# Cached keys turned by VectorE in 32x32 blocks instead of by TensorE, and fetched by one indirect transfer per slot from GpSimd's queue

## The reference

```python
D_MODEL, SEQ, DEC_BATCH, DEC_SEQ = 1024, 1024, 8, 4
PAST_LEN, PAGE_SIZE, N_HEADS, HEAD_DIM = 4096, 128, 8, 64      # 32 pages for each sample

def fox_sample(q, k, v, logf, k_past, v_past, logf_past):
    scale = HEAD_DIM ** -0.5
    d_new = lax.cumsum(logf, axis=1).transpose(0, 2, 1)
    rev = (lax.cumsum(logf_past, axis=1, reverse=True) - logf_past).transpose(0, 2, 1)
    sp = jnp.einsum('bqhd,bkhd->bhqk', q, k_past, preferred_element_type=jnp.float32) * scale
    sp = sp + d_new[:, :, :, None] + rev[:, :, None, :]
    ...  # sn: the same over the four new keys, causal
    p = jax.nn.softmax(jnp.concatenate([sp, sn], axis=-1), axis=-1)
    out = (jnp.einsum('bhqk,bkhd->bqhd', p[..., :n_past].astype(v_past.dtype), v_past)
           + jnp.einsum('bhqk,bkhd->bqhd', p[..., n_past:].astype(v.dtype), v))
```

## Time and profile before

| | |
|---|---|
| runs before | 2182.11, 2178.58, 2172.83 us, median 2178.58 us |
| profiled execution, span from first to last instruction | 2187.8 us |
| PE busy | 2010.4 us (92%) |
| DVE, ACT, POOL busy | 766.2 us (35%), 491.5 us (22%), 260.7 us (12%) |
| data moved | 458.72 MB, 210 GB/s over the span |
| from the scores of unit 0 to the end of slot 73 | 82.16 to 691.67 us |

### The profile page before, as it was taken

One profiled execution on the slowest core, in us unless ns is written; L12 is line 12 of the kernel. 1 busy time (PEld: TensorE's weight loads), 2 busy tenths in 40 slices (PEclk: granted clock), 3 DMA queues, 4 the chain that ended last, 5 costly groups with the idle time before them and its releaser, 6 DMA issues.

```text
span 2187.8 us, 34891 instructions
## 1 busy us (share of the span) xinstructions
PE 2010.4 (92%) x12990; PEld 1228.5 (56%) x12990; DVE 766.2 (35%) x1789; ACT 491.5 (22%) x1062; POOL 260.7 (12%) x402
## 2 busy tenths in 40 slices
PE   6999998989887999999999989998599999999994
PEld 4677765666654887788887446744333333333331
DVE  5221213555555572333333550623411111111115
ACT  3222222444331010111111021523122222221223
POOL 1101222322231000000000000000011111111110
PEclk9999999999998999999999999999799999999997
DMA  7546777987777022210111120304799999999976
GB/s 273 184 152 224 249 281 244 311 305 266 267 257 246 1 97 79 77 48 10 58 49 70 58 80 1 145 20 173 281 377 383 377 374 371 376 374 374 367 265 243
DMA packets 207153, 458.72 MB, mean 210 GB/s; under 512 B 18753, under 2 KB 48466, under 8 KB 206858
## 3 DMA queue, kind: packets, MB, share of 16 engines
q1 hardware_dynamic: 174410, 357.96, 46.4%
q0 software_dynamic: 32576, 98.53, 13.0%
HBM read 432.51 MB, written 32.17 MB: 212 GB/s over the span
## 4 chain that ended last, share of the span: by engine, by line
PE 82%; DMA 6%; DVE 4%; issue 3%; ACT 2%; SPq 2%; DVEq 1%; ACTq 0%; POOLq 0%
PE ps L1320 16%; PE ps L1625 10%; PE ps L1656 5%; PE ps L1380 5%; PE ps L1636 5%; PE ps L1121 5%; PE ps L1223 5%; PE ps L1409 4%; DMA kraw<-in_cache_k 3%; PE ps L1665 3%; PE ps L1093 3%; PE ps L1136 2%; PE ps L1498 2%; PE ps L1259 2%; PE ps L1234 2%
## 5 line engine op out<-in xcount | busy, mean ns | idle before, releaser
L1625 PE MATMUL ps<-gu,xgT 128*64 128x512 f32 x1024 | 228.5, 599 | 0.9 <-ACT xgT L1989 0.9
L1223 PE MATMUL ps<-consts,kraw 128*128 128x128 f32 x1024 | 141.6, 284 | 32.9 <-DMA kraw<-in_cache_k 27.7
L2985 POOL DMA_DIRECT2D vpage<-in_cache_v x232 | 125.0, 539 | 393.1 <-issue 385.2
L1320 PE MATMUL ps<-xnT,ring 128*128 128x264 f32 x672 | 162.1, 392 | 0.6 <-issue 0.6
L2264 DVE COPY kt<-ps 128x512 f32<-128x512 f32 x128 | 88.4, 691 | 202.6 <-PE ps L1223 201.9
L1223 PEld LDWEIGHTS ps<-consts,kraw 128*128 128x128 f32 x1024 | 116.3, 145 | 61.0 <-DMA kraw<-in_cache_k 30.7
L1625 PEld LDWEIGHTS ps<-gu,xgT 128*64 128x64 f32 x1024 | 71.1, 137 | 133.1 <-issue 130.0
L1320 PEld LDWEIGHTS ps<-xnT,ring 128*128 128x128 f32 x672 | 129.4, 193 | 23.8 <-issue 1.4
L1656 PE MATMUL ps<-wd,hidT_a 128*64 128x512 f32 x512 | 116.9, 598 | 19.6 <-ACT hidT_a L1999 12.7
L2874 DVE TENSOR_TENSOR sig_a<-ps,sig_a 128x256 f32<-128x256 f32 x32 | 13.6, 425 | 325.1 <-ACT sig_a L1993 325.1
L1762 ACT ACTIVATE kt<-ps 128x512 f32<-128x512 f32 x128 | 76.3, 596 | 191.9 <-PE ps L1223 190.0
(11 more groups left out here) (451 smaller groups left out, 3066.1 us busy)
## 6 DMA issues: line engine op xcount, KB each, us to landing
kraw<-in_cache_k SPq DMA_DIRECT2D x256, 256.0 KB, 4.1
gu<-in_w_expert_gate SPq DMA_DIRECT2D x32, 2048.0 KB, 23.4
gu<-in_w_expert_up SPq DMA_DIRECT2D x32, 2048.0 KB, 30.0
wd<-in_w_expert_down SPq DMA_DIRECT2D x31, 2048.0 KB, 8.3
vpage<-in_cache_v POOLq DMA_DIRECT2D x232, 256.0 KB, 4.9
ring<-in_w_in SPq DMA_DIRECT2D x12, 1024.0 KB, 9.1
yy<-y_d SPq DMA_DIRECT2D x16, 512.0 KB, 10.5
early<-in_w_in SPq DMA_DIRECT2D x6, 1024.0 KB, 10.1
```

Of the source, the lines that this page charges most:

```text
L1223: last = nc.tensor.transpose(bank(R.bank("kt", n, c))[:, j * PAGE:(j + 1) * PAGE], kraw[n % 2][:, j, c * P:(c + 1) * P], ident)
L1320: last = nc.tensor.matmul(bank(R.bank(name, f, q))[:, 0:QT], weight[:, k], src[:, k, cols], start=k == 0, stop=k == HK - 1)
L1625: last = nc.tensor.matmul(bank(0)[h * BA:(h + 1) * BA, :].rearrange("p (x n) -> p x n", x=2), src[:, k, 0:BA], weight[:, k, :, h * DE // 2 ...
L2985: pool.dma_start(vpage[value_place(n)][:, p, :], t["cache_v"][ds(page, 1)].rearrange("a s d -> (a s) d")).then_inc(v_in[value_place(n)], 16)
```

## The change

**Fetch.** `kraw[n % 2]` is filled by one indirect transfer on POOL's queue instead of four plain ones on SP's. A partition takes 8 KB in one piece: four consecutive tokens (c = 0..3) of all heads. Partition 32 j + s holds tokens 4 s to 4 s + 3 of page j. The row numbers `kidx` are loaded at the start by four small broadcasts and made by one DVE instruction.

**Turning.** `turn_keys` moves from PE to DVE: two instructions a unit, each turning 32x32 blocks of 128x1024 numbers from `kraw` into `kt`. The four tokens of a partition are interleaved again by the destination, so consecutive results lie 16 bytes apart. ACT and DVE no longer copy keys out of PSUM.

**Scores.** In `kt` the partitions 32 j to 32 j + 31 now hold 32 of a head's dimensions for page j's tokens, so the query operand is block-diagonal over the four pages (`qblk`, 32 columns, half of them zero), made for each sample by `spread_queries` (four small DVE copies). There are again 16 matmuls of 128x128 against 32 columns. A row of scores is now 4 x (head, query) + page instead of 32 x page + (head, query); `rev`, `sprob` and `snew` follow, and the sums over pages at the end are made on 8 partitions. The turned prompt probabilities are now all copied by ACT.

**Order.** POOL's list is now: keys of units 0 and 1, values of 0 and 1, keys 2 to 5, two small transfers for the new keys' terms, keys 6 to 13, and from then on values of n, keys of n+12. SP keeps the weights, `rev` and `negk`.

```diff
-        kt = [at(f"kt{s}", [P, KC, 4 * PAGE], a_ring + 16384 + s * 8192) for s in range(2)]
+        kt = [at(f"kt{s}", [P, NBLK, PAGE], a_ring + 16384 + s * 8192) for s in range(2)]
...
-        def load_keys(eng, n, p, page):
-
-            eng.dma_start(kraw[n % 2][:, p, :], t["cache_k"][ds(page, 1)].rearrange("a s d -> (a s) d")
-                          ).then_inc(k_in[n % 2], 16)
+        def load_keys(pool, n):
+
+            pool.indirect_dma_start(kraw[n % 2].rearrange("p c d -> p (c d)"), None,
+                                    t["cache_k"].rearrange("a (s c) d -> (a s) (c d)", c=4),
+                                    bass.IndirectOffsetOnAxis(ap=kidx[:, n:n + 1].bitcast(U32), axis=0)).then_inc(k_in[n % 2], 16)
...
             def sample_scores(n):
 
-                pe.wait_ge(side_ready, Q_READY)
-                R.read(pe, "kt", n, KC - 2), R.read(pe, "kt", n, KC - 1)
+                b = n // SU
+                pe.wait_ge(kt_ready, n + 1)
                 R.pe_free(pe, "sq", n)
-                for c in range(KC):
-                    for j in range(4):
-                        last = nc.tensor.matmul(bank(5)[j * QH:(j + 1) * QH, 0:PAGE], qnew[:, c, n // SU, :],
-                                                kt[n % 2][:, c, j * PAGE:(j + 1) * PAGE], start=c == 0, stop=c == KC - 1)
+                for x in range(4):
+                    first = x // 2 * 16
+                    for j in range(KC):
+                        last = nc.tensor.matmul(bank(5)[j * 32:(j + 1) * 32, 0:PAGE], qblk[b % 2][:, 2 * j + x % 2, first:first + 32],
+                                                kt[n % 2][:, 4 * j + x, :], start=x == 0, stop=x == 3)
                 last.then_inc(R.full, 1)
...
-            def copy_keys(n, c):
+            def turn_keys(n, half):
+
                 if n >= NSU:
                     return
-                if n >= 2:
-                    R.made(dve, "sq", n - 2)
-                R.made(dve, "kt", n, c)
-                nc.vector.tensor_copy(kt[n % 2][:, c, :], bank(R.bank("kt", n, c))).then_inc(R.by["dve"], 1)
+                if half == 0:
+                    dve.wait_ge(k_in[n % 2], 16 * (n // 2 + 1))
+                    if n >= 2:
+                        R.made(dve, "sq", n - 2)
+                last = nc.vector.transpose(
+                    kt[n % 2].rearrange("p e (s c) -> p c e s", c=4)[:, 2 * half:2 * half + 2],
+                    kraw[n % 2][:, 2 * half:2 * half + 2, :].rearrange("p c (e x) -> p c e x", x=32))
+                if half:
+                    last.then_inc(kt_ready, 1)
...
+            def keys(n0, n1):
+
+                for n in range(n0, min(n1, NSU)):
+                    if n >= 2:
+                        pool.wait_ge(kt_ready, n - 1)
+                    load_keys(pool, n)
...
             for n in range(VS, NSU):
                 load_values(n)
+                keys(n + 12, n + 13)
```

More of the change, by code:

```diff
@@ L488, in turn_groups @@
             n = UNITS[k][1] + 1
-            return [(g, 4 * g, min(4, n - 4 * g), "act" if (p + g) % 2 == 0 else "dve") for g in range(-(-n // 4))]
+            return [(g, 4 * g, min(4, n - 4 * g)) for g in range(-(-n // 4))]
         END = PROMPT0 + PROMPT_SLOTS
@@ L505, in add_probs @@
                 R.add("act", "st", b, r, banks=TURNS)
-        for n in range(2):
-            for c in range(KC):
-                add_keys(n, c)
         for n in range(NSU + LAG):
@@ L518, in build_program @@
                 R.add("dve", "po", NU - 1, banks=(4,))
-            for x, (k, p) in enumerate(halves(n)):
+            for k, p in halves(n):
                 if p == 0 and k:
@@ L893, in _ @@
             sp.dma_start(convp, t["convp"]).then_inc(tables_in, 16)
+            with nc.allow_non_contiguous_dma("page numbers, eight at a time"):
+                for j in range(4):
+                    sp.dma_start(kidx[j * 32:(j + 1) * 32, :].rearrange("p (b u) -> p b u", b=DB), t["pages"].rearrange(
+                        "a (b j u) -> a j b u", b=DB, j=4)[:, j].to_broadcast([32, DB, PAGES // 4])).then_inc(tables_in, 16)
             early_load(1, O_Q)
@@ L1248, in turn_sample_probs @@
                 R.pe_free(pe, "st", b, 2)
[L1249 removed]
+                nc.tensor.transpose(bank(R.bank("st", b, 2))[0:NS, 0:P], pnew[b % 2], ident).then_inc(R.full, 1)
             def weigh_pages(n):
@@ L1274, in pick_own @@
                 last.then_inc(R.full, 1)
-            for n in range(2):
-                turn_keys(n, range(KC))
             for n in range(NSU + LAG):
@@ L1290, in _ @@
                         prompt_scores(k + 1, p)
-                    if x == 0:
-                        turn_keys(n + 2, (2, 3))
                     turn_probs(k, p)
-                for x, item in enumerate(items(n)):
+                for item in items(n):
                     do_item(*item)
-                    if x == 0:
-                        turn_keys(n + 2, (2, 3))
-                if not halves(n) and not items(n):
-                    turn_keys(n + 2, (2, 3))
+                if n == 4:
+                    new_scores()
                 if n == 5:
-                    new_scores()
+                    spread_new()
                     pe.wait_ge(lf_ready, 1)
@@ L1860, in _ @@
                         exp_prompt(k + 1, 0)
-                for x, item in enumerate(items(n)):
+                for item in items(n):
                     copy_item(*item)
-                    if x == 0:
-                        copy_keys(n + 2, 2)
-                if not halves(n) and not items(n):
-                    copy_keys(n + 2, 2)
                 if KOUT0 <= n < KOUT0 + TILES:
@@ L2162, in _, with spread_queries @@
                                            ).then_inc(abs_ready, 1)
+            def spread_queries(b):
+                for g in range(4):
+                    rows = slice(g * 32, (g + 1) * 32)
+                    nc.vector.tensor_copy(
+                        qblk[b % 2].rearrange("p e (x q g) -> p e x q g", x=3, g=4)[rows, :, 0:3:2, :, g],
+                        qgrp[rows, :, :, :, b * DS:(b + 1) * DS].rearrange("p j e x q -> p (j e) x q"))
+                dve.drain()
             nc.vector.memset(qnew, 0.0)
-            nc.vector.memset(tops, NEG)
-            nc.vector.memset(sums, 0.0)
+            for p in range(2):
+                nc.vector.memset(qblk[p], 0.0)
             dve.drain()
             dve.wait_ge(qk_ready, 1)
+            for g in range(4):
+                for r in range(4):
+                    nc.vector.tensor_copy(qgrp[g * 32:(g + 1) * 32, :, r % 2, r // 2, :], qs[r * 32:(r + 1) * 32])
+            dve.drain()
+            spread_queries(0)
             for c in range(KC):
@@ L2294, in _ @@
                     join_scores(n)
-                copy_keys(n + 2, 1)
+                    if n % SU == 0 and n + SU < NSU:
+                        spread_queries(n // SU + 1)
+                turn_keys(n + 2, 0)
                 if n == PROMPT0 - 1:
```

220 lines of the change are left out of this document (102 added, 118 removed).

## The result

The changed kernel takes 2214.9 us (median of 4 runs, 2209.41 to 2217.52), the kernel before 2178.48 (4 runs, 2172.83 to 2182.11): ratio 1.0169, 95% interval 1.0139 to 1.0199. It is slower by 1.7%, a small but clear difference (the whole interval lies above 1), where 2095 us was forecast. The profiled execution has a span of 2215.8 us, 28.0 more than before.

The account below looks back on a forecast made before the run. PE was taken as the bound, transfers close behind. Gains of 25, 29 and 34 us in slots 0 to 13, 14 to 28 and 29 to 62, less 4 at the start, gave 84 us: about 2095 us, 8-in-10 range 2040 to 2150.

Parts of the forecast that it names:

- the paragraph on the new waits: Prompt slots: chain from values through keys, turning and prompt work takes 21.8 to 23.8 us for three slots, 7.3 to 7.9 each.
- The forecast's 245: Slots 29 to 62: predicted length 245 us, down from 279, a gain of 34.
- Slots 0 to 13: Slots 0 to 13: PE stays the bound, 129.4 - 25 = 104 us, gain 25.
- Slots 14 to 28: Slots 14 to 28: transfers 107 us, with 5% for three lists binding in turn 112 us, gain 29.
- the 107 us taken as the transfers' floor: Slots 14 to 28: a DMA share of 0.76 over 141.27 us taken as 107 us of work no edit removes.
- DVE's amount: Slots 29 to 62: DVE has 87 us of its own and 132 us of turning, 219 us.
- the allowance for coupling: Slots 29 to 62: 245 us taken, with PE 201, POOL 215, DVE 219, transfers 223 and the chain 248.
- rival 1 and 4: Turning on DVE: 2.7 us a half makes DVE the bound, 2125 us, chance 0.18; 4.9 a half, 2339, 0.10.
- rival 3: POOL becomes the bound at 7.6 us a slot, slots 29 to 62 about 282 us, total 2135; chance 0.10.
- (2): PE stays the bound, with faster 8 KB-row transfers and turning near 1.25 us: gain 125, total 2054 us; chance 0.15.
- the case that I gave 0.05: An order of waits not seen beforehand, of either sign, no size given; chance 0.05.
- signs of being wrong: Turning halves above 3.5 us, indirect transfers holding POOL several us, or late keys with PE's waits above 2 us a slot.

Follow-up runs that it names:

- numbers early alone: The change, with POOL reading its four page numbers ahead of its wait for `v_used`, both orders kept: 2173.9 us, ratio 0.9979 to the kernel before.
- half the values: The change with keys issued ahead of values on POOL, fetching only half of each value row from unit 2 on: 2113.2 us, ratio 0.9698.
- the last kernel of the table: The change with turning behind the prompt work, page numbers ahead of POOL's wait, and turned blocks written without the step: 2071.9 us, ratio 0.9518.
- the loop opened: The change with keys ahead of values on POOL (2128.4 us), turning behind the prompt work on DVE (2127.0), or both (2130.8).
- the turning last: The change with DVE's turning behind the slot's prompt work: 2127.0 us; with POOL's page numbers also ahead of its wait: 2103.1 us.
- the keys stood first: The change with keys of unit n+12 issued ahead of values of unit n on POOL: 2128.4 us, ratio 0.9771 to the kernel before.

## Why the prediction was wrong

- **The step that failed** is in the paragraph on the new waits: "PE needs that prompt work one slot later", and from it "21.8 to 23.8 us for three slots". The length was right, 23.5 us in the round above, in part by luck: its terms were off both ways (next point). But a slot with two halves has PE's `weigh_prompt(k)`, or its second pair of score products, in the same slot as DVE's `invert_sums(k)` or `biased`, which stand behind that slot's turning. PE needs them in this slot, not in the next, so the round spans two slots, and repeats: 17 rounds of 20.9 us on average make 354.7, where 34 slots of 7.3 us made 248. The forecast's 245 was short by 110 us, more than the whole gain. That every second slot has two halves stands in the kernel's list of halves, and I had averaged the prompt work over the slots (87/34) instead of laying out one slot of each kind.
- **Terms inside that chain.** Turning 3.8 (4 taken), values' numbers and issues 5.2 (4.6), prompt work behind the turning 0.6 (2.5), PE's part 5.0 (4 and 1). From the keys' issue to the turning it took 8.6 us, where 1.6 of issue and 4 to 6 to landing were taken: the values of the next unit (issued at 416.18) travel at the same time, and all three units shared one queue.
- **Start:** +4.2, as forecast. **Slots 0 to 13:** 20.0 instead of 25; 109.4 us. With numbers early alone they took 106.2: 3 us of the miss were late values: in slots 12 and 13 PE waited 4.1 us for `vpage` in the change, and 0.7 with numbers early.
- **Slots 14 to 28:** 33.6 instead of 29, with the transfers at 0.90. Fewer bytes shorten this stretch (97.5 us with half the values), but the 107 us taken as the transfers' floor was none: with the same bytes the last kernel of the table took 98.6.
- **DVE's amount** in slots 29 to 62, 218.6 against 219 forecast, and POOL's were right. What was wrong there is the allowance for coupling: with the loop opened the stretch took 267 to 271, not 245. It came under 245 only in kernels whose DVE had 50 to 60 us less to do (229.4 to 241.7); 2.2 us less a unit on POOL with the turning last made it 252.8.
- **The rivals:** turning was no slower than taken (rival 1 and 4 fall, 2.04 us), POOL was not the bound (rival 3: it stood 201.5 us before values), and PE neither (2). What happened was the case that I gave 0.05, an order of waits that I had not seen. One of the prediction's signs of being wrong was met: PE's waits for `diag` (64.7 us) and for the prompt's maxima (46.0) in slots 29 to 62 are 3.3 us a slot, and the clock fell behind them.
- **The stepped destination.** With the step 2.04 us and without 1.23 for 1024 columns, 2.0 and 1.2 ns a column. The Trainium skill (Vector Engine (DVE) Microarchitecture Reference, section 5.2) gives 1.71 ns a column for a destination that hops 4 KiB every element and 2.50 for a step of 24 words, both of a plain elementwise operation. That a step costs, the trace agrees; the 2.0 ns measured here for a block transpose with a step of four words lies between the two.

## What to carry to other kernels

Where a change puts a wait at the head of an in-order list, write out one round from an event to its own next occurrence, with the real order of the smallest and the largest slot, and divide by the slots that it spans; an average over slots hides the ones that decide. A loop through two lists opened at either of them, and a cheap edit of one link already helped (here, four register loads moved above a wait gave 41 us of the medians, 30.5 of them up to the end of the slots in the profiled executions), but mending two lists that wait on each other can move the wait instead of removing it. When an edit off the path moves transfers to fewer partitions, look at the DMA share beside the GB/s: here a share of 1.00 came with 218 GB/s, and 0.92 with 323.

## What the runs showed of the hardware

- Beside the transfers of the values, a transfer of 256 KB into 32 partitions (8 KB each) landed in 7.0 us (median), and the DMA engines stood at a share of 1.00 with 218 GB/s in slots 14 to 28; into 128 partitions (2 KB each) it landed in 4.1 us, at 0.92 with 323 GB/s.
- One indirect transfer of 128 rows costs POOL 1.03 us with rows of 8 KB, and the 0.99 us of the earlier trace rows with the expert stage's rows: the row's length doesn't show.
- Time with long waits was also time at a lower clock. In slots 29 to 62 PE's 2414 matmuls were busy 226.4 us at a granted clock of 0.79, and 207.8 us, with as many, at 0.89, once the keys stood first.
